# Bias rows into the input stage, five beside steps moved, and eight turning transfers on two queues, in a two-block kernel

## What is computed

```python
proj = rmsnorm(x) @ w_in                       # feature tiles 34..37 are the branch's input u
# state-space branch (s5_mixer): 32 groups of 16 channels, 64 complex states each
lam_bar = exp(lam * dt); b_bar = (lam_bar - 1) / lam * b
h = associative_scan(lam_bar * h + b_bar u)    # over the tokens
y = gelu(real(c h) + d * u); gl = y @ w_glu
y = gl[:, :512] * sigmoid(gl[:, 512:])
# dilated attention: bias = bias_tab[t5_bucket(distance)], a [4 x 384] row per group of heads
merged += sigmoid(xn @ w_gate[b]) * (y_b @ w_branch[b])      # for each of four branches
```

## Time and profile before

| what | value |
|---|---|
| median of 3 runs | 3575.17 us (3573.9 to 3576.09) |
| profiled execution, its own time | 3572.89 us |
| its span | 3571.2 us |
| instructions | 39536 |
| PE busy | 3412.1 us, 96% of the span |
| DVE, ACT, POOL busy | 55%, 38%, 13% |

### The profile page before, as it was taken

The page is one execution under the profiler, slowest core; times in us unless marked ns, Lnnn a source line. Parts: engine busy times, 40 slices in busy tenths (PEclk is TensorE's granted clock), DMA queues, the critical chain, the costliest instruction groups (busy, mean ns, idle before and its releaser), DMA issues.

```text
span 3571.2 us, 39536 instructions
## 1 busy us (share of the span) xinstructions
PE 3412.1 (96%) x16130; PEld 2770.9 (78%) x16130; DVE 1965.6 (55%) x2371; ACT 1356.3 (38%) x1880; POOL 461.3 (13%) x325
## 2 busy tenths in 40 slices
PE   7999999999899899999999999999899989999998
PEld 4778887877777578888888877777698768888886
DVE  7454452233554434687773264444576678888335
ACT  3232112333145733433331146353545454444213
POOL 0000000000001000344540010000000035554000
PEclk9999999999999999999999999999999999999999
DMA  3213241112410013233238322120203312333732
GB/s 111 61 38 123 97 165 60 48 48 81 139 51 27 27 51 112 95 112 111 107 122 320 112 83 92 59 100 30 95 1 124 118 71 106 113 112 140 309 105 83
DMA packets 114390, 353.82 MB, mean 99 GB/s; under 512 B 16009, under 2 KB 25993, under 8 KB 114193
## 3 DMA queue, kind: packets, MB, share of 16 engines
q1 hardware_dynamic: 114208, 351.28, 28.1%
HBM read 268.15 MB, written 81.91 MB: 98 GB/s over the span
## 4 chain that ended last, share of the span: by engine, by line
PE 82%; DVE 8%; ACT 7%; issue 1%; DMA 1%; SPq 0%; ACTq 0%; DVEq 0%
PE PS L491 41%; PE PS L2334 21%; PE PS L474 8%; PE PS L3678 1%; PE PS L1817 1%; PE PS L3690 1%; PE PS L2809 1%; ACT whi L431 1%; DVE wlo L436 1%; PE PS L1526 1%; ACT dS L1580 1%; PE PS L503 1%; PE PS L918 1%; PE PS L1839 1%; PE PS L509 1%
## 5 line engine op out<-in xcount | busy, mean ns | idle before, releaser
L436 DVE TENSOR_TENSOR wlo<-raw,whi 128x1024 fp32r<-128x1024 f32 (+3 forms) x393 | 499.1, 1271 | 443.9 <-ACT whi L431 441.3
L431 ACT CAST whi<-raw 128x1024 fp32r<-128x1024 f32 (+3 forms) x393 | 372.4, 948 | 745.4 <-PE PS L491 337.1
L491 PE MATMUL PS<-xhi,whi 128*128 128x512 f32 x1904 | 617.6, 406 | 32.5 <-DVE xlo L525 12.8
L491 PE MATMUL PS<-xlo,whi 128*128 128x512 f32 x1904 | 594.7, 394 | 0.0
L491 PE MATMUL PS<-xhi,wlo 128*128 128x512 f32 x1904 | 592.2, 392 | 0.0
L491 PEld LDWEIGHTS PS<-xhi,whi 128*128 128x128 f32 x1904 | 355.3, 191 | 123.5 <-issue 28.6
L491 PEld LDWEIGHTS PS<-xlo,whi 128*128 128x128 f32 x1904 | 362.2, 190 | 78.0
L491 PEld LDWEIGHTS PS<-xhi,wlo 128*128 128x128 f32 x1904 | 361.5, 190 | 77.8
L2334 PE MATMUL PS<-tf,whi 128*128 128x512 f32 x936 | 288.2, 389 | 1.7 <-DVE wlo L436 1.7
L2334 PE MATMUL PS<-xhi,whi 128*128 128x512 f32 x624 | 243.8, 391 | 7.2 <-DVE xlo L2319 5.6
L2334 PE MATMUL PS<-xlo,whi 128*128 128x512 f32 x624 | 243.5, 390 | 0.0
(11 more groups left out here) (553 smaller groups left out, 5554.2 us busy)
## 6 DMA issues: line engine op xcount, KB each, us to landing
raw<-in_w_up SPq DMA_DIRECT2D x88, 512.0 KB, 3.4
hid<-hs SPq DMA_DIRECT2D x88, 512.0 KB, 3.6
raw<-in_w_in SPq DMA_DIRECT2D x67, 512.0 KB, 3.2
slot<-hid SPq DMA_DIRECT2D x56, 512.0 KB, 6.5
adr<-in_w_ada SPq DMA_DIRECT2D x48, 512.0 KB, 4.5
raw<-in_w_down SPq DMA_DIRECT2D x48, 512.0 KB, 3.5
raw<-in_w_gate SPq DMA_DIRECT2D x32, 512.0 KB, 3.3
merged<-hid SPq DMA_DIRECT2D x16, 512.0 KB, 12.8
```

The source lines that it names most:

```text
L431: act.e.copy(whis[i % RING][:, ks, :], raws[i % RING][:, ks, :]).then_inc(*give("w_hi", i))
L436: dve.e.tensor_tensor(wlos[i % RING][:, ks, :], raws[i % RING][:, ks, :], whis[i % RING][:, ks, :].bitcast(F32), ALU.subtract).then_inc(*g ...
L491: ins = pe.e.matmul(ps[:, h * 512:(h + 1) * 512], w[s][:, k, :], x[:, h * 512:(h + 1) * 512], start=(at == 0 and n == 0), stop=(at == kt - ...
```

## The change

The three transfers that the bias rows need move into the input stage, behind the third weight load; the three matmuls go behind the sum of squares, their DVE additions before the first `weights_lo`, and the store before the fifth load. DVE no longer waits for that store before it makes `CL`; ACT waits for it before it writes `Ks`. The slot "cl" has 5 steps in place of 10; the rest falls to "glu", so every slot between them starts 5 step numbers earlier. Of the eight turning transfers SP issues four (q = 0..3) and ACT four (q = 4..7), on its own queue.

```diff
--- before.py
+++ after.py
@@ -547,7 +547,15 @@
             sp.e.dma_start(cpos, A["c_tpos"][:, 0:128]).then_inc(*land("c_pos"))
             for k in range(8):
                 sp.e.dma_start(X[:, k, :], A["xT"][:, k, :]).then_inc(*land(f"lane{k}", "x"))
-            for i in range(6):
+            for i in range(3):
+                load_weights(sp, i)
+            sp.e.dma_start(hot, A["c_hot"]).then_inc(*land("c_hot"))
+            sp.e.dma_start(pen, A["c_pen"]).then_inc(*land("c_pen"))
+            sp.e.dma_start(relb, A["rel_bias"]).then_inc(*land("c_relb"))
+            load_weights(sp, 3)
+            sp.wait_ge("bias_row", 2)
+            sp.e.dma_start(bsc, brow).then_inc(*land("bsc"))
+            for i in range(4, 6):
                 load_weights(sp, i)
 
         def input_pe(pe):
@@ -556,6 +564,12 @@
             for k in range(8):
                 pe.wait_ge("x_sq", k)
                 sum_over_partitions(pe, ps, xtmp[k % 3], k == 0, k == 7, "x_ss", k)
+            rows_ring = [2, 3]
+            for g in range(3):
+                ps = psum.take(pe, rows_ring, f"bias{g}", ("bias_row", g))
+                pe.wait_ge("c_hot")
+                pe.wait_ge("c_relb")
+                pe.e.matmul(ps[0:4, 0:384], relb[:, 4 * g:4 * g + 4], hot[:, 384 * g:384 * g + 384], start=True, stop=True).then_inc(*give("bias_mm", g))
 
         def input_act(act):
             for k in range(8):
@@ -578,6 +592,10 @@
             dve.e.memset(ones, 1.0).then_inc(*give("c_ones"))
             dve.e.memset(epsc, EPS).then_inc(*give("c_eps"))
             s5_powers(dve)
+            for g in range(3):
+                dve.wait_ge("bias_mm", g)
+                dve.wait_ge("c_pen")
+                dve.e.tensor_tensor(brow[:, g, :], psum.of(f"bias{g}")[0:4, 0:384], pen[:, 384 * g:384 * g + 384], ALU.add).then_inc(*give("bias_row", g))
             for i in range(3):
                 weights_lo(dve, i)
             for k in range(9):
@@ -759,7 +777,7 @@
 
         BESIDE = [("w_in", 36), ("w_in", 37)] + [("w_gate", 8 * b + ft) for b, ft in EARLY_S5]
         BESIDE0 = PLAN.index(("w_in", 36, 0, 8))
-        SLOTS = [("cl", 10), ("k", 3), ("ks", 6)]
+        SLOTS = [("cl", 5), ("k", 3), ("ks", 6)]
         for hf in range(2):
             SLOTS += [(f"ut{hf}{fl}{x}", 1) for fl in range(2) for x in range(2)] + [(f"wt{hf}{n}", 1) for n in range(2)]
             SLOTS += [(f"turn{hf}", 8), (f"sin{hf}", 8), (f"rot{hf}", 8)]
@@ -821,20 +839,18 @@
                     sp.wait_ge("gate", ft // 8, ft % 8)
                     sp.e.dma_start(spill[:, 18 + ft, :], g_early).then_inc(*land("gate_out", ft // 8, ft % 8))
 
+        def s5_rows(by, q, signal):
+            by.e.dma_start(Mk[16 * q:16 * q + 16, :, 16 * q:128], Ks[:, :, 0:128 - 16 * q]).then_inc(*land(signal, q))
+
         def s5_sp(sp):
             begin_sp(sp, "w_in", 34)
             begin_sp(sp, "w_in", 35)
-            sp.e.dma_start(hot, A["c_hot"]).then_inc(*land("c_hot"))
-            sp.e.dma_start(pen, A["c_pen"]).then_inc(*land("c_pen"))
-            sp.e.dma_start(relb, A["rel_bias"]).then_inc(*land("c_relb"))
-            sp.wait_ge("bias_row", 2)
-            sp.e.dma_start(bsc, brow).then_inc(*land("bsc"))
             beside_sp(sp, "cl")
             beside_sp(sp, "k")
             sp.wait_ge("s5_ks", 1, 1)
             sp.wait_ge("s5_mzero")
-            for q in range(8):
-                sp.e.dma_start(Mk[16 * q:16 * q + 16, :, 16 * q:128], Ks[:, :, 0:128 - 16 * q]).then_inc(*land("s5_mk", q))
+            for q in range(4):
+                s5_rows(sp, q, "s5_mk")
             for name, _ in SLOTS[2:]:
                 beside_sp(sp, name)
             for f in range(4):
@@ -853,12 +869,6 @@
             pA, pB = [2], [3]
             product(pe, ring, "w_in", 34, XN, ("s5_u", 0))
             product(pe, ring, "w_in", 35, XN, ("s5_u", 1))
-            for g in range(3):
-                ps = psum.take(pe, rows_ring, f"bias{g}", ("bias_row", g))
-                pe.wait_ge("c_hot")
-                pe.wait_ge("c_relb")
-                pe.e.matmul(ps[0:4, 0:384], relb[:, 4 * g:4 * g + 4], hot[:, 384 * g:384 * g + 384], start=True, stop=True).then_inc(*give("bias_mm", g))
-
             beside("cl")
             for hf in range(2):
                 pk = [psum.take(pe, (pA, pB)[gl], f"s5k{hf}{gl}", ("s5_ks", hf, gl)) for gl in range(2)]
@@ -936,11 +946,17 @@
             u_tile(0)
             u_tile(1)
             beside_act(act, "cl")
+            act.wait_ge("bsc")
             for hf in range(2):
                 for gl in range(2):
                     act.wait_ge("s5_kmm", hf)
                     g = slice(16 * hf + gl, 16 * hf + 16, 2)
                     act.e.copy(Ks[:, g, :], psum.of(f"s5k{hf}{gl}")[0:16, :].rearrange("p (a b) -> p a b", a=8)).then_inc(*give("s5_ks", hf, gl))
+                if hf:
+                    act.wait_ge("s5_ks", 1, 1)
+                    act.wait_ge("s5_mzero")
+                    for q in range(4, 8):
+                        s5_rows(act, q, "s5_mk2")
                 beside_act(act, "ks" if hf else "k")
             for hf in range(2):
                 for fl in range(2):
@@ -991,13 +1007,8 @@
             ts, tt, stt, cp = s5_small(dve)
             begin_dve(dve, "w_in", 34)
             begin_dve(dve, "w_in", 35)
-            for g in range(3):
-                dve.wait_ge("bias_mm", g)
-                dve.wait_ge("c_pen")
-                dve.e.tensor_tensor(brow[:, g, :], psum.of(f"bias{g}")[0:4, 0:384], pen[:, 384 * g:384 * g + 384], ALU.add).then_inc(*give("bias_row", g))
             flat4 = lambda x: x.rearrange("p a b c -> p (a b c)")
             beside_dve(dve, "cl")
-            dve.wait_ge("bsc")
             for hf in range(2):
                 ii = slice(8 * hf, 8 * hf + 8)
                 full = [128, 8, 9, 16]
@@ -1016,7 +1027,8 @@
                 beside_dve(dve, "ks" if hf else "k")
             for n in range(2):
                 dve.e.memset(H[n][:, :, 0:1], 0.0).then_inc(*give("s5_hz", n))
-            dve.wait_ge("s5_mk", 7)
+            dve.wait_ge("s5_mk", 3)
+            dve.wait_ge("s5_mk2", 7)
             dve.wait_ge("s5_cl", 1)
             for hf in range(2):
                 if hf:
```

## The result

| | median | range | runs |
|---|---|---|---|
| before | 3576.02 us | 3572.84 to 3578.73 | 14 |
| after | 3583.32 us | 3578.42 to 3586.04 | 14 |

The ratio is 1.0019, 95% interval 1.0012 to 1.0027: the change makes the kernel 7.3 us (0.19%) slower where I forecast 3.4. It lies inside the range 3569 to 3585, near its upper end, and outside my own narrower range of 3574 to 3582. It is also clear of zero: the interval is about 3 us wide to either side, so my "not to be told from no change" and "0.2% is about what a measurement can tell" were too cautious. The profiled executions, after and before, span 3579.9 and 3571.2 us, 8.7 apart.

A forecast was written before the change was run, and what follows sets the result against it. PE was taken to bound the kernel (82% of the chain that ended last). -7.2 + 2.6 + 8.0 = +3.4 us, added to the median 3575.17, gave 3578.6 us; range 3569 to 3585, own range 3574 to 3582.

The forecast's parts named there:

- Parts 1 and 2: Input stage and "cl": bias rows moved at cost 0, PE 4.8 us earlier; CL half 0 from 60.2, no PE wait.
- Part 3: In "k": weight 4's rounding falls behind the Ks copies; PE waits 8.3 us for CL half 1, restart +2.3 us.
- Part 4: The turning: two queues take 13 us instead of 15.55, ACT's issues cost 0; bu of half 0 shifts by -7.2 us.
- the first rival: The turning: two queues bring nothing, 15.55 us stays, PE waits 4 us for w; 3582 to 3583 us, chance 0.20.
- Part 5: Second half, "ut": gate 5 now stands on ACT ahead of the WT copies; PE waits +2.6 us (2 to 3.5).
- Part 6: "glu": weight 14 comes only after gate 9, so the first ylo is late before the w_glu products: +8.0 us.
- both slow rivals: Two queues bring nothing, 3582 to 3583 us, 0.20; ACT's queue and the second-half wait cost more, 3583 us, 0.12.
- the second: Slow rival: ACT late at the transposes, second-half wait long enough for the clock to fall: +4.3 us, 3583 us, 0.12.

The follow-up runs named there:

- e1: The changed kernel with slot "cl" at 10 steps again, bias rows in the input stage and two queues kept: 3565.67 us, 0.9975 of before.
- e3: The changed kernel with ACT's event 'begin p = 0' (rounding of weight 4) at step number 4 instead of 6: 3572.07 us, 0.9990 of before.
- e2: The changed kernel with all eight turning transfers on SP: 3583.28 us, 1.0021 of before.
- e4: The changed kernel with ACT's event 'end p = 5' (gate 5) at 51 instead of 49, behind both WT copies: 3575.26 us, 0.9994 of before.
- e5: The changed kernel with 'begin p = 9' at 75 and 'begin p = 10' at 80 on ACT and DVE: 3578.36 us, 1.0009 of before.
- e7: The changed kernel with "ks" 8 steps, "glu" 8, three events renumbered on ACT, one also on DVE, two queues: 3556.67 us, 0.9944 of before.
- e8: e7 with all eight turning transfers on SP: 3556.09 us, 0.9947 of before.
- e6: The kernel before with only the bias rows' loads, matmuls, additions and store moved to the input stage: 3567.79 us, 0.9980 of before.
- e9: e6 with the state-space stage's ring of PSUM pairs started as [3, 2] instead of [2, 3]: 3569.61 us, 0.9985 of before.

## Why the prediction was right, and where it was off

**Parts 1 and 2** held. The first L572 (the bias matmul's new line) came at 25.58, the additions ended at 28.4, `CL` half 0 started at 60.85 and PE had no wait before the first `kmm`. Everything was 0.8 us late from the sum of squares on; e1, with the same input stage, was 0.1 us late behind its second product (its copy of U at 63.21 against 63.10), so this is the execution, not the edit.

**Part 3**, the step that I held for decisive, held: the wait is 8.3 us, forecast and measured. e3 shows that it is caused by where ACT rounds weight 4, and e1 that the slot number put it there. That the second `kmm` ends at 91.8 where I had 91.9 is luck: it began 0.85 us late (86.85 against 86.0), and its restart cost 1.3 us (5.0 us in place of 3.6) where I took 2.3. Behind the same 8.3 us wait it took 6.6, 6.4 and 6.4 us in e2, e4 and e5.

**Part 4** is where the forecast was first too low. I took 13 us for two queues, between 9.0 and 15.55; it was 15.1, near the upper bound. e2, e7 and e8 show that the second queue shortens nothing, so the first rival, which names the Trainium skill's page, was right in its mechanism. The share wasn't free capacity: it was 0.65 with either number of queues. The lower bound of 9.0 also mixed two stretches, the share of 101 to 113.5 (0.58) with the length of the whole turning, whose own share is 0.70. And ACT's four issues, which I put at up to 7 us or more and whose cost to PE I took as 0, took 10.1 us; PE waited 3.6 us for the copy behind them and restarted at half clock (0.51 from 107.5 to 110). `bu` came 5.0 us earlier instead of 7.2. e2 shows that this blocked queue wasn't a loss of its own: without it PE waits 3.3 us for w.

**Part 5** had the mechanism right and the size wrong: +2.6 forecast, +5.9 measured (`bu` of half 0 is 5.0 earlier than before, the last gelu's end, 264.38 and 265.29, 0.9 later). Of the 3.3 that lack, 2.9 are the restart (`bu` 6.5 us instead of 3.6; 5.1 to 6.1 in e2, e3 and e5, so this profile shows the largest). The start of `bu` itself moved by 3.1 against the 2.6 of the forecast; the store's landing took 193.31 - 188.36 = 4.95 us where I took 4.1, and smaller terms went the other way. The 2.1 us of PE's old wait at these transposes went unseen in the sum, and rightly gave nothing here: PE ran ahead and waited longer for `WT`, which hangs on DVE. e4 shows it all given back: from `bu` of half 0 to `bu` of half 1 it is 71.8 us there, 77.2 after and 74.1 before.

**Part 6**: +8.0 forecast, 275.77 - 267.00 = 8.8 less 0.9 of earlier shift = 7.9 measured. e5's trace shows the cause.

The sum: -5.0 + 5.9 + 7.9 = +8.8 of span against my +3.4. So the direction and the three waits were right, and two terms were sized too low: the turning with its restart by 2.2 us, the second half by 3.3. The time is that of both slow rivals (3582 to 3583, 0.20, and 3583, 0.12), and the mechanism takes from both: the two queues that bring nothing from the first, ACT's late copy and the restart in the second half from the second. They aren't exclusive, as I had treated them, and their terms belonged in the forecast.

Why a change with two real gains loses: bias rows 5 us, the ring 2 us (e6). The five steps moved from "cl" to "glu" should have covered another wait; but they renumbered every event between, and three of these fell behind something late: weight 4 behind `Ks` (about 10 us, e3), gate 5 before `WT` (9 us, e4), gate 9 before weight 14 (4 us by the medians, 7 by the trace, e5). The three add up to more than the 16 us of e1 because the moved steps do cover other waits (e8 is 10 us faster than e1). Put right, and with two steps more in "ks", the same idea is 19 us faster than before (e8).

## What to carry to other kernels

Where several engines share one numbered schedule, a number changed for one engine's cover moves all engines' events: list, for every slot, which waits of the other engines now stand ahead of which instruction, before counting the cover. An in-order engine should get an event that only needs old data (a weight rounding) ahead of its next wait on the critical chain, and one that needs a late store behind it. Splitting transfers of many short runs over two issuing engines puts issue time on the second engine's compute queue (10.1 us on ACT here); where the transfers themselves are the bound, as in e2 and e8, nothing comes back.

## What the runs showed of the hardware that I had not expected

Eight `Mk` transfers of short runs took 15.0 us by one queue and 15.1 by two, though the 16 engines' mean share was under 0.7 in both. The issue itself was long: eight took 13.1 us of SP's queue in e2. Four of them (q = 4 to 7) issued from ACT alone took 4.3 us of its queue in e1, and 10.1 us beside SP's four, which took 7.0. What bounds the transfers below a full share was not found. The Trainium skill, DMA: Bandwidth & Descriptors, section Issuing engines are not separate DMA queues, says that transfers from several issuing engines share the same 16 DMA engines, and that a second issuing engine saves only issue time, usually small beside the transfer. These runs agree that it brings no faster transfer; the issue time wasn't small here, and what the longer queue saved of it (13.1 to 10.1 us) brought nothing.

The same wait costs restarts of different size. In e6 and e9, both with 3.9 us before the `w_glu` products, the clock in the 3 us from there was 0.61 and 0.50 (columns as above):

```profile
261.00:264.00 3.00, 3.00 (x9) 2.38 (x10) 3.00 (x3) 0.21 (x1) 0.00 (x0) 0.61 0.65 242
```

```profile
264.00:267.00 3.00, 3.00 (x8) 2.32 (x9) 3.00 (x3) 0.22 (x1) 0.00 (x0) 0.50 0.65 242
```

In e6 the clock was still 1.00 when PE began again at 260.89 and fell about half a microsecond later; in e9 it was 0.50 before PE began at 263.81. From there to DVE's copy of the first product it is 7.35 us in e6 and 8.4 in e9, against 5.8 in e7 and e8, where PE doesn't wait for `ylo`. The second `kmm` after its 8.3 us wait took 5.0 us in one profile and 6.6 in another. Single profiles of these kernels therefore differ by 1 to 2 us at one restart where nothing was changed.
